# The last 64 tokens of the two output projections: both column halves at once, in two 64-column tiles of TensorE's array

## What is computed

```
x = x + concatenate([y_s5, y_lru]) @ w_out          # 1088 x 1024 by 1024 x 1024
x = x + (attention output o) @ w_o                  # 1088 x 1024 by 1024 x 1024
x = x + hier_moe(rmsnorm(x))                        # router, top-2 of 32 experts
```

## Time and profile before

| | |
|---|---|
| median of 3 runs | 1330.39 us (1329.91 to 1332.71) |
| the profiled execution's own time | 1330.93 us |
| its span, first to last instruction | 1329.2 us |
| busy, PE / weight loads / DVE / ACT / POOL | 1184.3 / 665.9 / 496.6 / 251.4 / 82.2 us |
| mean granted TensorE clock | 0.931 |

### The profile page before, as it was taken

One profiled execution on the slowest core, in us unless ns is written; L12 is line 12 of the kernel. 1 busy time (PEld: TensorE's weight loads), 2 busy tenths in 40 slices (PEclk: granted clock), 3 DMA queues, 4 the chain that ended last, 5 costly groups with the idle time before them and its releaser, 6 DMA issues. The chain is left out here.

```text
span 1329.2 us, 14902 instructions
## 1 busy us (share of the span) xinstructions
PE 1184.3 (89%) x6205; PEld 665.9 (50%) x6205; DVE 496.6 (37%) x1008; ACT 251.4 (19%) x524; POOL 82.2 (6%) x104
## 2 busy tenths in 40 slices
PE   6999999999999999999999899999479999999910
PEld 4566666777544446666667554554333333333300
DVE  3494799377422220002544403222621221121146
ACT  4200312456310001001222101000100111011122
POOL 4000100010000000000000000000011111111100
PEclk9999999999999999999888779999589999999965
DMA  8019310765440003001131363000349999999556
GB/s 268 24 55 151 36 10 32 221 235 189 158 146 0 0 0 127 1 0 64 64 121 70 127 243 142 37 37 24 158 152 381 402 400 399 397 410 393 193 198 230
DMA packets 65365, 209.24 MB, mean 157 GB/s; under 512 B 13560, under 2 KB 22416, under 8 KB 57072
## 3 DMA queue, kind: packets, MB, share of 16 engines
q1 hardware_dynamic: 54528, 177.68, 38.0%
q0 software_dynamic: 10640, 30.55, 6.5%
q10 hardware_dynamic: 128, 0.03, 0.0%
HBM read 187.05 MB, written 28.53 MB: 162 GB/s over the span
## 5 line engine op out<-in xcount | busy, mean ns | idle before, releaser
L713 PE MATMUL bank<-arena 128*128 128x512 f32 (+1 forms) x576 | 252.3, 597 | 1.0 <-DVE arena L1468 0.7
L566 PE MATMUL bank<-arena 128*128 128x360 f32 (+1 forms) x576 | 179.8, 474 | 2.9 <-DMA arena<-in_w_in 1.9
L713 PEld LDWEIGHTS bank<-arena 128*128 128x128 f32 (+1 forms) x576 | 105.4, 185 | 135.9 <-issue 134.4
L883 PE MATMUL bank<-arena 128*32 128x512 f32 x1536 | 169.8, 594 | 0.0
L566 PEld LDWEIGHTS bank<-arena 128*128 128x128 f32 x576 | 110.3, 193 | 69.3 <-issue 3.8
L731 PE MATMUL bank<-arena 128*128 128x360 f32 (+1 forms) x384 | 117.4, 468 | 0.0
L964 ACT ACTIVATE arena<-bank 128x360 f32<-128x360 f32 (+7 forms) x125 | 52.8, 424 | 319.9 <-PE bank L566 130.5
L883 PEld LDWEIGHTS bank<-arena 128*32 128x32 f32 x1536 | 47.5, 110 | 104.6 <-issue 104.6
L1492 DVE TENSOR_TENSOR arena<-arena,bank 128x512 f32<-128x512 f32 (+1 forms) x36 | 24.7, 687 | 191.8 <-PE bank L713 191.8
L731 PEld LDWEIGHTS bank<-arena 128*128 128x128 f32 x384 | 72.8, 190 | 43.7
L899 PE MATMUL bank<-arena 128*32 128x512 f32 x768 | 86.8, 592 | 0.6 <-ACT arena L1139 0.6
(11 more groups left out here) (354 smaller groups left out, 1247.6 us busy)
## 6 DMA issues: line engine op xcount, KB each, us to landing
arena<-in_w_gate SPq DMA_DIRECT2D x32, 1024.0 KB
arena<-in_w_up SPq DMA_DIRECT2D x32, 1024.0 KB
arena<-in_w_down SPq DMA_DIRECT2D x32, 1024.0 KB, 12.9
arena<-in_ck SPq DMA_DIRECT2D x8, 1024.0 KB, 4.9
arena<-in_cv SPq DMA_DIRECT2D x8, 1024.0 KB, 7.1
arena<-work_moe SPq DMA_DIRECT2D x16, 512.0 KB, 5.5
arena<-in_w_in SPq DMA_DIRECT2D x3, 2048.0 KB, 14.6
arena<-in_x SPq DMA_DIRECT2D x8, 512.0 KB, 7.7
```

Of the source, the lines that this page charges most:

```text
L566: last = nc.tensor.matmul(b[:, 0:w], win[slot][:, k, m * P:m * P + P], ht[:, k, c0:c0 + w], start=k == 0, stop=k == KD - 1)
L713: last = nc.tensor.matmul(b[0:ROWS[i], :], lhs(k, i), w[0][:, k, nh * 512:nh * 512 + 512], start=k == 0, stop=k == KD - 1)
L883: last = nc.tensor.matmul(bank[2 + j % 2][t0:t0 + QT, :].rearrange("p (h n) -> p h n", h=2), xgt[j % 2][:, k, t0:t0 + QT], gu[e % GUB][:, ...
```

## The change

For the tile with fewer than 128 rows, `resid` on PE claims both banks first. It then goes over `k` on the outside and over the column half on the inside, so that matmuls of the two halves alternate. The left half goes to partitions 0 to 63 of bank 4, as before; the right half goes to partitions 64 to 127 of bank 5, and with that to the other 64 columns of the array. DVE reads the right half from partitions 64 to 127. The number of matmuls, weight loads and additions stays the same. Both calls of `resid` are changed, so the code runs twice.

```
             def resid(i, lhs, w):
                 if i == 0:
                     pe.wait_ge(sem[w[1]], w[2])
+                if ROWS[i] < P:
+                    bs = [claim(MD, md, "md_free") for nh in range(2)]
+                    for k in range(KD):
+                        for nh in range(2):
+                            last = nc.tensor.matmul(bs[nh][64 * nh:64 * nh + 64, :], lhs(k, i), w[0][:, k, nh * 512:nh * 512 + 512], start=k == 0, stop=k == KD - 1)
+                            if k == KD - 1:
+                                last.then_inc(sem["md_full"], 1)
+                    return
                 for nh in range(2):
                     b = claim(MD, md, "md_free")
...
-                    V.tensor_tensor(xs_, xs_, bank[MD[n % 2]][0:r, :], ADD).then_inc(sem["md_free"], 1)
+                    p0 = 64 * nh if r < P else 0
+                    V.tensor_tensor(xs_, xs_, bank[MD[n % 2]][p0:p0 + r, :], ADD).then_inc(sem["md_free"], 1)
```

## The result

| | before | after |
|---|---|---|
| median of 6 runs each | 1331.53 us (1329.91 to 1334.17) | 1318.58 us (1315.16 to 1323.64) |
| ratio, 95% interval | | 0.9904 (0.9881 to 0.9926) |
| the profiled execution's own time, its span | 1330.93, 1329.2 us | 1318.20, 1316.4 us |
| mean granted clock | 0.931 | 0.932 |

The account below looks back on a forecast made before the run. PE was taken as the bound through tile 8, then DVE's chain, then PE again. Two gains of 6.88 us less 0.68 and 0.05 give 13.0 us, so 1330.39 becomes 1317.4 us, range 1314.5 to 1321.5.

Parts of the forecast that it names:

- The packing's gain: Tile 8's `resid` matmuls on PE: two column tiles share each 0.43 us step, 7.07 us instead of 13.95.
- the partial overlap: Rival at tile 8: L640's rate of 1.58 holds, 8.8 us a tile, 1320.9 us in all; chance 0.07.
- Weight loads: Tile 8's LDWEIGHTS, 0.14 us each, two in a 0.43 us step: costed at nothing, covered by running matmuls.
- The second claim: PE waits for bank 5 before tile 8's first matmul: 0.05 us in the first projection, nothing in the second.
- The two additions: DVE adds both halves of tile 8 after PE's end: 0.68 us later in the second projection, hidden in the first.
- What moved with it: Cache loads (at about 490.6 us) and expert weights 3 and 4 are triggered earlier; from there the old trace, shifted.
- The sum: Whole program: 2 x 6.88 - 0.68 - 0.05 = 13.0 us gained, 1317.4 us for the median.
- The clock's spread: Granted clock's falls and rises shifting by one or two microseconds against the program's steps: 2.5 us either way.
- The exposed loads: Rival at tile 8: a load can't start while the other tile streams, 11.4 us, 1325.9 in all; chance 0.01.
- no overlap: Rival at tile 8: 32 steps remain and the additions cost 0.7 us, 1331.1 us in all; chance 0.05.
- slower: Rival at tile 8: matmuls one after another with uncovered loads, 18.2 us, 1339.7 in all; chance 0.02.
- The two reasons for no overlap: Tile 8's two tiles read different moving columns and write different banks, unlike packed matmuls in the trace; either might separate them.

Follow-up runs that it names:

- The order without the second tile: The change, but both alternating halves use array columns 0 to 63 and DVE reads partitions 0 to 63 for both; 1330.67 us, ratio 1.0008 to the kernel before.
- the two reordered kernels: Second projection: router(7) ahead of tile 8's transposes, tile 7's gain ahead of tile 8's normalisation; on the change 1314.64 us, on the kernel before 1327.50 us.

## Why the prediction was right

**The packing's gain** was taken from `gate_up` at 6.88 us a call. It measured 13.95 - 7.09 = 6.86 in both projections. The row with four 32-column tiles priced two 64-column tiles to 0.02 us, and the factor is 1.97. The L640 rate of 1.58 did not come back, and with it falls the partial overlap. The prediction misread that row. Sixteen records of L640 take 1.15 us, without a stop after eight; the next twelve are

```profile
145.35 0.92 PE L640 MATMUL bank<-arena 128*64 128x136 f32 x12 [0.90 <-ACT arena L964]
```

Four records more, two pairs, take 1.15 - 0.92 = 0.23 us. That is 0.115 us for a pair, as long as the 0.114 us that I reckoned for one record. So the pairs of L640 overlapped in full within a group, and the factor of 1.58 came from setting times with each group's start and tail in them against one without. The Trainium skill, "TensorE: Matmul & The Clock Gate", section "Measured speedup vs the span model", had given 1.59 by my estimate. By its span model its figure holds one matmul's whole duration. Here 16 steps share one tail: 16 x 0.43 + 0.2 = 7.1 us.

**Weight loads** were costed at nothing, and they cost nothing. In the Trainium skill, the same page's section "The mechanism" lists that a load overlaps running matmuls only in another row group. These loads used all 128 rows, came two in each step of 0.43 us, and did not lengthen it. The trace disagrees with that line. The same section of the Trainium skill also lets a load go early into a background weight buffer, which these rows would fit; no view here shows where a load goes.

**The second claim** was put at 0.05 us. From the transposes to tile 8 in the first projection it is 1.03 us, against 483.46 - 482.49 = 0.97: 0.06 more. The order without the second tile, which also claims both banks first, has 1.03 too (485.62 - 484.59), so the 0.06 go with the claim and not with the packing. In the second projection it is free, as predicted (from tile 7's last addition to tile 8's matmuls 904.65 - 902.18 = 2.47 us, and 910.16 - 907.69 = 2.47 before).

**The two additions** were put at 0.68 us on the path, with 0.2 either way, hidden in the first projection. Hidden they were. In the second PE's wait grew by 2.60 - 1.69 = 0.91 us: 1.40 - 0.68 = 0.72 for the addition, and 0.2 for DVE's lost head start behind it. This term was mis-sized by 0.23 us, just outside the 0.2 allowed, because I priced the read from partitions 64 to 127 by its own length and not by what follows it.

**What moved with it.** The cache loads came at 492.16 us, not 490.6. They stand 7.13 us behind the start of tile 8, where they stood 13.98; tile 8 itself started 1.57 us later, for reasons ahead of the change. The experts took nothing back that stands clear of their own spread: from the transposes of tile 8's normalised rows to the end it is 398.9 to 404.1 us in the five profiles where the second projection's tile 8 takes 7.09 us, and 397.4 to 401.4 in the four where it takes longer (the two reordered kernels left out).

**The sum** was 13.0 us; by its own terms 2 x 6.86 - 0.91 - 0.06 = 12.75 came out, and 12.73 was measured in the two places. That the median fell within 1.2 us of 1317.4 is partly luck: the interval on the gain is 3 us either way, and the median of the kernel before was 1331.53 us over six runs, 1.1 more than the value that I subtracted from. **The clock's spread** was put at 2.5 us either way for the whole. Single executions spread wider, over 8.5 us in the six of the change, and a second profile of it shows two half-clock stretches in the experts, where I had counted on none. The median fell inside the range regardless.

**The rivals.** The exposed loads are ruled out by the loads' rows, no overlap and slower by 7.09 us. The two reasons for no overlap fall with it, and the trace of before spoke against both already. L640 takes `uch[:, 2 * gp + l, :]`, another moving operand for each of its two tiles, and not a shared one as I wrote. The pairs at L629, which split the array by rows and not by columns, write two banks, and four of their records take 0.39 us where one lasts 0.27: the second pair adds 0.12 us, where 0.43 x 128/512 = 0.107 would be one record's.

## What to carry to other kernels

In this kernel a matmul whose weights fill only 64 of the array's columns costs as much as a full one (13.95 us a call against 13.90), and a second one rides along free if it goes to the other columns and the two streams alternate in the queue (7.09 us for both halves). Putting them in other columns is not enough: PE started the second stream only four records ahead (12.26 us). Packed streams end together, so look at who drains them: that drain comes later by one bank's read, and what waits for it should have other work moved into the gap. A rate from a short group has its start and its tail in it; compare two groups of different length instead. Here full overlap looked like 1.58 because of them.

## What the runs showed that I had not expected

- With the two halves one after the other in the queue but on different columns, the second began four float32 records, two matmuls, before the first's end: 12.26 us instead of 13.95.
- A DVE addition that reads partitions 64 to 127 took no longer than one from 0 to 63 (1.40 us for the pair), but DVE's next read of a bank, from partition 0, then lost its head start of 0.16 to 0.2 us on the instruction before it. With the last read from partitions 0 to 63, or a full tile's, it kept it.
- In the experts the granted clock fell to 0.50 for 3.4 us at 1120.9 and again at 1196.0 us in one profile, each time behind a wait of 2.5 us of PE for gathered rows, and not in another of the same kernel, whose longest such wait was 2.25 us. A wait of 2.65 us in the kernel before brought no fall. What decides it is open.
- Work of PE moved ahead of a clock fall is cheaper by itself: router(7) took about 2 us at a granted clock of 1.00 and 3.56 at 0.50.
